# Norm statistics by a 128x128 block of ones, with root and reciprocal taken over all token columns in PSUM

## The chip, the cores and the metric

The kernel runs on one core of a Trainium2 chip. The metric is device time in microseconds (us) of one launch, and lower is better. The core has a matrix engine (TensorE, PE in the profile; its weight loads are PEld), VectorE (DVE), ScalarE (ACT), GpSimd (POOL) and SyncE (SP), which here issues the transfers. Each engine works through its own list of instructions in order and waits for the others only at semaphores.

## What is computed

A two-layer backbone over 512 latent tokens and 256 context tokens, 1024 features wide, all in fp32. The layers are built from the same step, a root-mean-square norm with a gain, followed by a scale and a shift that depend on the conditioning vector:

```python
def rms_norm(x, g):
    xf = x.astype(jnp.float32)
    y = xf * lax.rsqrt(jnp.mean(xf * xf, axis=-1, keepdims=True) + EPS)
    return (y * g.astype(jnp.float32)).astype(x.dtype)

def modulate(x, g, shift, scale):
    return rms_norm(x, g) * (1 + scale) + shift

for l in range(DEPTH):                     # DEPTH = 2
    ...
    a_lat = modulate(x, norm1_g[l], mod_lat[0], mod_lat[1])
    a_ctx = modulate(h, norm1_g[l], mod_ctx[0], mod_ctx[1])
    m_lat, m_ctx = token_mixers(a_lat, a_ctx, ...)
    x = x + mod_lat[2] * m_lat
    x = x + mod_lat[5] * sq_relu_mlp(modulate(x, norm2_g[l], mod_lat[3], mod_lat[4]), w_ff1[l], w_ff2[l])
    ...
```

So there are four norms: before the input projection and before the MLP, in each of two layers. The last one has no context tokens, since the output holds latent tokens only.

## The kernel before

The residual stream stands in `X`, 128 features on the partitions, 8 feature tiles (`KT`), and 768 token columns (`COLS`: 512 latent, `LAT`, then 256 context). Weights come in fp32 units of 128x1024 (`raw`); ACT rounds each to a high part (`Whi`), POOL subtracts to get the low part (`Wlo`), and every product is three matmuls: high by high, high by low, low by high. The activations are split the same way into `Ahi` and `Alo`, by the norm itself.

The order on each engine is written out by hand. The four norms are numbered n = 0 to 3. Each goes through the same chain:

- ACT squares each feature tile of `X` into `sqb` (L562). DVE adds the first seven squares into one tile, `sq_sums`, a part of `Ab` (`sq_add`, L868); the eighth stays in `sqb`.
- PE sums over the 128 features on the partitions (`stats`, `token_sums`, L1249). The squares are the stationary operand, 128 tokens at a time, and a 128x1 column of ones is the moving one; the result is one PSUM column per token tile, tokens on the partitions: `psS` 128x6, or 128x4 in the last norm. This is done for `sq_sums` and again for `sqb`.
- ACT takes the root of these 128x6 values (L568), DVE the reciprocal (L838), both in the small tile `rstd`.
- PE spreads them back to token columns that are the same on all partitions: one transpose per token tile of a column broadcast to 128x128 (`spread`, L1234 with `rstd`), latent tokens into the PSUM bank `ps6`, context tokens into `ps7`.
- DVE multiplies each feature tile of `X` by its gain and by `ps7` or `ps6` (L855 for 256 context columns, L857 for 512 latent ones). ACT adds the shift and rounds to `Ahi` (L575, L576), and DVE (even tiles, L844 and L846) or POOL (odd tiles, L457) makes `Alo`. The first matmul of the next stage (L1353, or L1566 in the MLP) waits for the first `Alo`.

`ps6` and `ps7` also serve the modulation vectors. PE writes partial sums there (`mod_sums`), DVE reduces them (`mod_reduce`, L822 and L825) and counts `mod_evac`. Before, `spread` waits for that count, since it is the first of the norm's steps that writes these banks. Before norm 1 the last `mod_reduce` stands on DVE behind the last `sq_add` and ahead of the reciprocal.

Of the kernel before, what the change touches and what calls it, by code (L numbers as in the profile page):

```python
# [17 lines left out]
P = 128  # L18
D, DEPTH, LAT, CTX = 1024, 2, 512, 256
KT = D // P  # L20
NT, NL = (LAT + CTX) // P, LAT // P
COLS = LAT + CTX
# [33 lines left out]
def build(nc, a):  # L56
    fp32, f32r = mybir.dt.float32, mybir.dt.float32r
    ALU, ACT, AX = mybir.AluOpType, mybir.ActivationFunctionType, mybir.AxisListType.X
# [3 lines left out]
    def sb(name, shape, dt=fp32):  # L62
        return stack.enter_context(nc.sbuf_tensor(name, shape, dt))
# [37 lines left out]
    Whi = sb("Whi", [P, 2, UE], f32r)  # L101
    Wlo = sb("Wlo", [P, 2, UE], f32r)
    ident = sb("ident", [P, P])
    ones = sb("ones", [P, 1])
    rstd = sb("rstd", [P, 2, NT])
    warm = sb("warm", [P, 1])
    identr = sb("identr", [P, P], f32r)
    maskr = sb("maskr", [P, 2, P], f32r)
# [30 lines left out]
    epst = sb("epst", [P, 1])  # L139


    def pb(name, n):
        return stack.enter_context(nc.psum_tensor(name, [P, n], fp32))

    psA, psB, psS = pb("psA", 1024), pb("psB", 1024), pb("psS", 1024)
    pair = [psA, psB]
    ps6, ps7 = pb("ps6", 512), pb("ps7", 512)
    tokbank = [psA[:, 0:512], psA[:, 512:1024], psB[:, 0:512], psB[:, 512:1024], psS[:, 0:512], psS[:, 512:1024]]

    names = """consts_in x_in tmp_in stored rows_T par_ready csil_ready mod_pe mod_first mod_used mod_step modp_ready mod_red mod_evac xT_ready x_ready  # L150
        stat_sq stat_done sq_sum rt_sqrt rstd_ready rb_ready dve a_full a_hi a_lo_even a_lo_odd hi_done lo_done unit_done proj_ready p_ready qk_var qk_sqrt
        q_ready k_ready rq_ready rk_ready tr_ready tr_evac za_evac zb_evac zc_evac y_ready y_hi y_lo
        kz_ready kv_ready st_ready sc_ready md_ready sd_zero xq_ready gg_ready rot_step ret_ready g_cent g_sq g_gate g_var g_sqrt g_inv v_sum v_ready ro_ready rT_ready rT_hi rT_lo
        kq_hi kl_ready kl_zero qb_hi qb_lo s_ready s_max s_exp pt_ready pt_evac pv_ready es_in es_out ao_ready aoT_ready aoT_hi aoT_lo
# [2 lines left out]
    S = {n: stack.enter_context(nc.semaphore(n)) for n in names}  # L157
# [5 lines left out]
    evac_index, n = {}, 0  # L163
# [4 lines left out]
    TT = [NT, NL]  # L168
# [366 lines left out]
    def _(act):  # L535
# [28 lines left out]
        def norm(n, cols):  # L564

            l, g = n // 2, n % 2
            act.wait_ge(S["stat_done"], n + 1)
            nc.scalar.activation(rstd[:, 0, 0:cols // P], psS[:, 0:cols // P], ACT.Sqrt, scale=1.0 / D, bias=epst[:, 0:1]).then_inc(S["rt_sqrt"], 1)  # L568
            for k in range(KT):
                act.wait_ge(S["a_full"], 8 * n + k + 1)  # L570
                sh = modT[:, l, 24 * g + k, :]
                for dst in (Ahi[:, k, :], norm_at(k)) if k % 2 else (Ahi[:, k, :],):

                    if cols > LAT:
                        nc.scalar.activation(dst[:, LAT:cols], norm_at(k)[:, LAT:cols], ACT.Identity, bias=sh[:, 1:2])  # L575
                    last = nc.scalar.activation(dst[:, 0:LAT], norm_at(k)[:, 0:LAT], ACT.Identity, bias=sh[:, 0:1])  # L576
                last.then_inc(S["a_hi"], 1)
# [204 lines left out]
    def _(dve):  # L782
        V = nc.vector
# [50 lines left out]
        def norm(l, k, cols):  # L834

            n = 2 * l + k
            dve.wait_ge(S["rt_sqrt"], n + 1)
            V.reciprocal(rstd[:, 1, 0:cols // P], rstd[:, 0, 0:cols // P]).then_inc(S["rstd_ready"], 1)  # L838

            def low(j):  # L840
                dve.wait_ge(S["a_hi"], 8 * n + j + 1)
                x, sh = norm_at(j), modT[:, l, 24 * k + j, :]
                if cols > LAT:
                    V.scalar_tensor_tensor(out=Alo[:, j, LAT:cols], in0=x[:, LAT:cols], scalar=sh[:, 1:2], in1=Ahi[:, j, LAT:cols],  # L844
                                           op0=ALU.add, op1=ALU.subtract)
                V.scalar_tensor_tensor(out=Alo[:, j, 0:LAT], in0=x[:, 0:LAT], scalar=sh[:, 0:1], in1=Ahi[:, j, 0:LAT],  # L846
                                       op0=ALU.add, op1=ALU.subtract).then_inc(S["a_lo_even"], 1)

            dve.wait_ge(S["rb_ready"], n + 1)
            for j in range(KT):  # L850
                if j >= 4 and j % 2:
                    dve.wait_ge(*a_lo(n, j - 4))
                x = norm_at(j)
                if cols > LAT:
                    V.scalar_tensor_tensor(out=x[:, LAT:cols], in0=X[:, j, LAT:cols], scalar=gs[:, l, k, j, 1:2], in1=ps7[:, 0:cols - LAT],  # L855
                                           op0=ALU.mult, op1=ALU.mult)
                V.scalar_tensor_tensor(out=x[:, 0:LAT], in0=X[:, j, 0:LAT], scalar=gs[:, l, k, j, 0:1], in1=ps6[:, 0:LAT],  # L857
                                       op0=ALU.mult, op1=ALU.mult).then_inc(S["a_full"], 1)
                if j % 2:
                    low(j - 1)  # L860
# [369 lines left out]
    def _(pe):  # L1230
        mm = nc.tensor.matmul

        def tr(out, in_, n=P):
            return nc.tensor.transpose(out, in_, ident[0:n, 0:n])  # L1234

        def mod_sums(used, w, wd, acc):

            pe.wait_ge(used, w + 1)
            pe.wait_ge(S["mod_step"], wd * 3 + 3)
            for s, ps in ((0, ps6), (1, ps7)):  # L1240
                for t in range(4):
                    last = tr(ps[:, t * P:(t + 1) * P], acc[:, s, t * P:(t + 1) * P])
            last.then_inc(S["modp_ready"], 1)

        def token_sums(n, squares, tiles_, first, last_):

            for t in range(tiles_):

                ins = mm(psS[:, t:t + 1], squares[:, t * P:(t + 1) * P], ones[:, :], start=(first and t == 0), stop=(last_ and t == tiles_ - 1))  # L1249
            return ins  # L1250

        def stats(n, tiles_):

            pe.wait_ge(S["sq_sum"], 6 * n + 6)
            token_sums(n, sq_sums, tiles_, True, False)
            pe.wait_ge(S["stat_sq"], 8 * n + 8)
            token_sums(n, sqb[:, 1], tiles_, False, True).then_inc(S["stat_done"], 1)

        def spread(n, tiles_):

            pe.wait_ge(S["rstd_ready"], n + 1)
            for t in range(tiles_):
                last = tr(ps6[:, t * P:(t + 1) * P] if t < NL else ps7[:, (t - NL) * P:(t - NL + 1) * P], rstd[:, 1, t:t + 1].to_broadcast([P, P]))
            last.then_inc(S["rb_ready"], 1)

        def fourier_weights(l):

# [37 lines left out]
        for m in range(KT):  # L1305
            if m >= 2:
                pe.wait_ge(S["x_ready"], m - 1)
            for t in range(NT):
                last = tr(pair[m % 2][:, t * P:(t + 1) * P], Xin[:, t, m * P:(m + 1) * P])
# [5 lines left out]
                mod_sums(S["mod_first"], 3, 3, maccs[0])  # L1315
        pe.wait_ge(S["mod_evac"], 1)
        mod_sums(S["mod_first"], 7, 7, maccs[1])
        stats(0, NT)
        pe.wait_ge(S["mod_evac"], 4)

        for l in range(DEPTH):
            u0, uf = l * UL, l * UL + UP + UO
            tiles = proj_tiles(l)
            pe.wait_ge(S["prep_wd"], 2 * l + 2)
            spread(2 * l, NT)

            for u in range(UP):
                g = u // 4
                n = GROUPS[g][1]
# [241 lines left out]
            for u in range(UO):  # L1571
# [5 lines left out]
                if l == 0 and u in (5, 7):  # L1577
# [1 line left out]
                    i = u // 2 - 2  # L1579
                    pe.wait_ge(S["mod_evac"], 10 + i)  # L1580
                    mod_sums(S["mod_used"], LATE - MOD0 + 4 * i + 3, 32 + 4 * i + 3, maccs[i])
            stats(2 * l + 1, TT[l])
            if l == 0:
                pe.wait_ge(S["mod_evac"], 12)
            spread(2 * l + 1, TT[l])


            pe.wait_ge(S["lo_done"], uf + 2)
            for k in range(KT):
# [53 lines left out]
            for k in range(4):  # L1643
                uu = uf + 60 + k
                pe.wait_ge(S["lo_done"], uu + 1)
                for o in range(2):
# [4 lines left out]
                    offs = [i * 256 + o * P for i in range(CHUNK)]  # L1651
                    tile(pair[m % 2], uu % 2, offs, Hhi[:, 1], Hlo[:, 1]).then_inc(S["lin_ready"], 1)
            if l == 0:
                stats(2, NT)

        pe.wait_ge(S["resid_done"], 144)
# [78 lines left out]
```

## Time and profile before

| what | value |
|---|---|
| median of 3 runs | 1805.34 us (1792.31 to 1811.72) |
| profiled execution, its own time | 1804.67 us |
| its span | 1802.9 us |
| PE busy | 1653.7 us, 92% |
| DVE busy | 1071.2 us, 59% |
| ACT busy | 572.3 us, 32% |
| POOL busy | 565.0 us, 31% |

PE is busy for nearly all of the span, so its gaps are what other engines can lose or save. The chain that ended last gives PE 56%, "issue" 19%, DVE 15% and ACT 4%. A norm is one of the few places where PE stands idle while a short chain of the other engines runs.

### The profile page before, as it was taken

To read this page: it belongs to the slowest core of one execution; us is meant where nothing else is said; L and a number is where in the kernel's file an instruction comes from. 1 tells how busy PE (TensorE), PEld (TensorE's weight loads), DVE (VectorE), ACT (ScalarE), POOL (GpSimd) and SP (SyncE) were. 2 spreads that over 40 slices of the span, in tenths; PEclk is the share of its full clock that TensorE was granted. 3 is DMA by queue.
4 is the path that set the end of the run, shared out by engine and by line. 5 is a ranking of instruction groups with operands and counts; after the bars stand their busy time and mean duration, and the time that the engine had idled before them with its cause. 6 is when DMAs were issued, how large, how long until landed. Compare 5 with 4: busy or idle time off the path is not lost.

```text
span 1802.9 us, 23460 instructions
## 1 busy us (share of the span) xinstructions
PE 1653.7 (92%) x8944; PEld 1425.2 (79%) x8944; DVE 1071.2 (59%) x1534; ACT 572.3 (32%) x912; POOL 565.0 (31%) x312
## 2 busy tenths in 40 slices
PE   6799778998979998998999997998899899999998
PEld 6678567897868887887888886887798678888887
DVE  3779975554856775766677437368453554444442
ACT  1531133563142121221211215323364442222221
POOL 0234546101232222222222233335301344444442
PEclk9999889898989998999999997998699899999999
DMA  7254411001413433444244111222000233333332
GB/s 269 70 168 146 130 36 42 1 1 36 135 60 104 129 105 96 133 116 125 71 140 117 59 59 37 83 80 71 1 1 24 70 94 94 93 93 93 93 93 93
DMA packets 159407, 156.08 MB, mean 87 GB/s; under 512 B 6336, under 2 KB 123728, under 8 KB 159312
## 3 DMA queue, kind: packets, MB, share of 16 engines
q1 hardware_dynamic: 159312, 154.72, 28.3%
q8 instruction: 70, 1.15, 0.3%
q14 instruction: 25, 0.20, 0.0%
HBM read 152.61 MB, written 2.10 MB: 86 GB/s over the span
## 4 chain that ended last, share of the span: by engine, by line
PE 56%; issue 19%; DVE 15%; ACT 4%; POOL 3%; DMA 2%; SPq 0%; POOLq 0%; DVEq 0%; ACTq 0%
PE psA L1566 18%; PE psB L1566 17%; PE ps L1535 4%; POOL Wlo L430 3%; PE psS L1234 2%; DVE Tb L813 2%; DVE scr L968 2%; DVE macc L813 2%; PE psS L1294 1%; PE ps L1234 1%; PE psS L1459 1%; DMA modraw<-in_w_mod_dram 1%; DVE Ab L1174 1%; PE psS L1249 1%; DVE scr L962 1%
## 5 line engine op out<-in xcount | busy, mean ns | idle before, releaser
L430 POOL TENSOR_TENSOR Wlo<-raw,Whi 128x1024 fp32r<-128x1024 f32 x172 | 419.1, 2437 | 1075.0 <-ACT Whi L541 1075.0
L541 ACT ACTIVATE Whi<-raw 128x1024 fp32r<-128x1024 f32 x180 | 190.8, 1061 | 782.2 <-PE psB L1566 329.6
L1174 DVE TENSOR_TENSOR Ab<-Tb 128x768 f32<-128x768 f32 (+1 forms) x64 | 162.0, 2531 | 189.3 <-ACT Tb L750 189.3
L813 DVE SCALAR_TENSOR_TENSOR macc<-modraw,csil,macc 128x512 f32<-128x512 f32 x224 | 193.3, 925 | 8.3 <-DMA modraw<-in_w_mod_dram 8.2
L1566 PE MATMUL psA<-Ahi,Whi 128*128 128x512 f32 x480 | 150.2, 368 | 21.8 <-POOL Wlo L430 9.1
L1566 PE MATMUL psA<-Ahi,Wlo 128*128 128x512 f32 x480 | 148.5, 364 | 3.4 <-issue 3.4
L1566 PE MATMUL psA<-Alo,Whi 128*128 128x512 f32 x480 | 148.2, 363 | 0.0
L1566 PE MATMUL psB<-Ahi,Whi 128*128 128x512 f32 x480 | 145.0, 356 | 0.0
L1566 PE MATMUL psB<-Ahi,Wlo 128*128 128x512 f32 x480 | 144.7, 355 | 0.0
L1566 PE MATMUL psB<-Alo,Whi 128*128 128x512 f32 x480 | 144.5, 355 | 0.0
L1566 PE MATMUL psA<-Hhi,Whi 128*128 128x512 f32 (+1 forms) x384 | 117.2, 359 | 14.0 <-DVE X L951 14.0
L1566 PE MATMUL psA<-Hhi,Wlo 128*128 128x512 f32 (+1 forms) x384 | 115.4, 355 | 0.0
L1566 PE MATMUL psA<-Hlo,Whi 128*128 128x512 f32 (+1 forms) x384 | 115.4, 354 | 0.0
L1566 PE MATMUL psB<-Hhi,Wlo 128*128 128x512 f32 (+1 forms) x384 | 115.4, 354 | 0.0
L1566 PE MATMUL psB<-Hlo,Whi 128*128 128x512 f32 (+1 forms) x384 | 115.3, 354 | 0.0
L1566 PE MATMUL psB<-Hhi,Whi 128*128 128x512 f32 (+1 forms) x384 | 115.2, 354 | 0.0
L1566 PEld LDWEIGHTS psA<-Ahi,Whi 128*128 128x128 f32 x480 | 82.0, 196 | 37.7 <-issue 14.7
L752 ACT ACTIVATE Hhi<-Ab 128x768 fp32r<-128x768 f32 (+1 forms) x64 | 47.4, 740 | 166.2 <-DVE Ab L1174 166.2
L1566 PEld LDWEIGHTS psA<-Ahi,Wlo 128*128 128x128 f32 x480 | 81.8, 195 | 17.9 <-issue 4.2
L1566 PEld LDWEIGHTS psA<-Alo,Whi 128*128 128x128 f32 x480 | 81.8, 195 | 14.0
L951 DVE SCALAR_TENSOR_TENSOR X<-psA,modT,X 128x512 f32<-128x512 f32 x72 | 53.5, 744 | 65.8 <-PE psA L1566 65.8
L1566 PEld LDWEIGHTS psB<-Alo,Whi 128*128 128x128 f32 x480 | 79.4, 189 | 13.5
(293 smaller groups left out, 3311.6 us busy)
## 6 DMA issues: line engine op xcount, KB each, us to landing
raw<-in_w_ff_dram SPq DMA_DIRECT2D x128, 512.0 KB, 4.1
modraw<-in_w_mod_dram SPq DMA_DIRECT2D x80, 512.0 KB, 4.1
raw<-in_w_in_dram SPq DMA_DIRECT2D x36, 512.0 KB, 3.7
modst<-in_w_mod_dram SPq DMA_DIRECT2D x16, 512.0 KB, 5.2
raw<-in_w_out_dram SPq DMA_DIRECT2D x16, 512.0 KB, 4.0
modraw<-in_dft_lat_dram SPq DMA_DIRECT2D x8, 257.0 KB, 3.6
Xin<-in_x_dram SPq DMA_DIRECT2D x4, 512.0 KB, 10.1
out_dram<-outs SPq DMA_DIRECT2D x4, 512.0 KB, 3.0
```

What stands on the lines that cost most here:

```text
L430: nc.gpsimd.tensor_tensor(Wlo[:, s, :], raw[:, s, :], Whi[:, s, :], ALU.subtract).then_inc(S["lo_done"], 1)
L541: nc.scalar.activation(Whi[:, slot, :], raw[:, slot, :], ACT.Copy).then_inc(S["hi_done"], 1)
L752: nc.scalar.activation(Hhi[:, hpar, k, 0:CW[l]], Ab[:, k % 2, 0:CW[l]], ACT.Copy).then_inc(S["h_hi"], 1)
L813: ins = V.scalar_tensor_tensor(out=acc[:, s, :], in0=src[:, kk * MCH:(kk + 1) * MCH], scalar=col, in1=acc[:, s, :], op0=ALU.mult, op1=ALU.add)
L951: V.scalar_tensor_tensor(out=X[:, m, 0:LAT], in0=pair[p][:, 0:LAT], scalar=modT[:, l, 8 * chunk + m, 0:1], in1=X[:, m, 0:LAT], op0=ALU.mul ...
L962: link(V.tensor_tensor(scr[:, 1, 0:n].rearrange("p (h d) -> p h d", h=nh), v3, bc(C, 1, [P, nh, HD]), ALU.mult))
L968: link(V.tensor_tensor(os[:, :, q, f, :], vs[:, :, q, 1 - f, :], bc(ss[:, q, f, :], 1, [P, nh, i]), ALU.mult))
L1174: V.tensor_tensor(Ab[:, k % 2, 0:w], Tb[:, k % 2, 0:w], Tb[:, k % 2, 0:w], ALU.mult).then_inc(S["h_full"], 1)
L1234: return nc.tensor.transpose(out, in_, ident[0:n, 0:n])
L1249: ins = mm(psS[:, t:t + 1], squares[:, t * P:(t + 1) * P], ones[:, :], start=(first and t == 0), stop=(last_ and t == tiles_ - 1))
L1535: last = mm((ps6, ps7)[b % 2][:, h * HD:(h + 1) * HD], PTs[:, it % 2, i * P:(i + 1) * P], Pk[:, kt, P + (h // 4) * HD:P + (h // 4 + 1) * H ...
L1566: last = mm(dst[:, c0:c0 + cn], wt, x[:, i, c0:c0 + cn], start=f, stop=e)
```

## The change

The column of ones becomes a 128x128 block of ones, and the operands of the statistics matmuls change places: the ones are stationary, and the squares are streamed as 512 latent and 256 context columns. Each output column then holds its token's sum on all 128 partitions, straight in `ps6` and `ps7`. The root (ACT) and the reciprocal (DVE) are taken in place over all of these columns, and the spreading transposes, their semaphore `rb_ready` and the tile `rstd` go. As the statistics now write `ps6` and `ps7`, the waits for `mod_evac` and `prep_wd` that stood ahead of `spread` stand ahead of `stats`.

```diff
--- before.py
+++ after.py
@@ -101,8 +101,7 @@
     Whi = sb("Whi", [P, 2, UE], f32r)
     Wlo = sb("Wlo", [P, 2, UE], f32r)
     ident = sb("ident", [P, P])
-    ones = sb("ones", [P, 1])
-    rstd = sb("rstd", [P, 2, NT])
+    ones = sb("ones", [P, P])
     warm = sb("warm", [P, 1])
     identr = sb("identr", [P, P], f32r)
     maskr = sb("maskr", [P, 2, P], f32r)
...
@@ -565,7 +564,9 @@
 
             l, g = n // 2, n % 2
             act.wait_ge(S["stat_done"], n + 1)
-            nc.scalar.activation(rstd[:, 0, 0:cols // P], psS[:, 0:cols // P], ACT.Sqrt, scale=1.0 / D, bias=epst[:, 0:1]).then_inc(S["rt_sqrt"], 1)
+            if cols > LAT:
+                nc.scalar.activation(ps7[:, 0:cols - LAT], ps7[:, 0:cols - LAT], ACT.Sqrt, scale=1.0 / D, bias=epst[:, 0:1])
+            nc.scalar.activation(ps6[:, 0:LAT], ps6[:, 0:LAT], ACT.Sqrt, scale=1.0 / D, bias=epst[:, 0:1]).then_inc(S["rt_sqrt"], 1)
             for k in range(KT):
                 act.wait_ge(S["a_full"], 8 * n + k + 1)
                 sh = modT[:, l, 24 * g + k, :]
@@ -835,7 +836,9 @@
 
             n = 2 * l + k
             dve.wait_ge(S["rt_sqrt"], n + 1)
-            V.reciprocal(rstd[:, 1, 0:cols // P], rstd[:, 0, 0:cols // P]).then_inc(S["rstd_ready"], 1)
+            if cols > LAT:
+                V.reciprocal(ps7[:, 0:cols - LAT], ps7[:, 0:cols - LAT])
+            V.reciprocal(ps6[:, 0:LAT], ps6[:, 0:LAT]).then_inc(S["rstd_ready"], 1)
 
             def low(j):
                 dve.wait_ge(S["a_hi"], 8 * n + j + 1)
@@ -846,7 +849,7 @@
                 V.scalar_tensor_tensor(out=Alo[:, j, 0:LAT], in0=x[:, 0:LAT], scalar=sh[:, 0:1], in1=Ahi[:, j, 0:LAT],
                                        op0=ALU.add, op1=ALU.subtract).then_inc(S["a_lo_even"], 1)
 
-            dve.wait_ge(S["rb_ready"], n + 1)
+            dve.wait_ge(S["rstd_ready"], n + 1)
             for j in range(KT):
                 if j >= 4 and j % 2:
                     dve.wait_ge(*a_lo(n, j - 4))
@@ -1244,10 +1247,9 @@
 
         def token_sums(n, squares, tiles_, first, last_):
 
-            for t in range(tiles_):
-
-                ins = mm(psS[:, t:t + 1], squares[:, t * P:(t + 1) * P], ones[:, :], start=(first and t == 0), stop=(last_ and t == tiles_ - 1))
-            return ins
+            if tiles_ > NL:
+                mm(ps7[:, 0:COLS - LAT], ones[:, :], squares[:, LAT:COLS], start=first, stop=last_)
+            return mm(ps6[:, 0:LAT], ones[:, :], squares[:, 0:LAT], start=first, stop=last_)
 
         def stats(n, tiles_):
 
@@ -1255,13 +1257,6 @@
             token_sums(n, sq_sums, tiles_, True, False)
             pe.wait_ge(S["stat_sq"], 8 * n + 8)
             token_sums(n, sqb[:, 1], tiles_, False, True).then_inc(S["stat_done"], 1)
-
-        def spread(n, tiles_):
-
-            pe.wait_ge(S["rstd_ready"], n + 1)
-            for t in range(tiles_):
-                last = tr(ps6[:, t * P:(t + 1) * P] if t < NL else ps7[:, (t - NL) * P:(t - NL + 1) * P], rstd[:, 1, t:t + 1].to_broadcast([P, P]))
-            last.then_inc(S["rb_ready"], 1)
 
         def fourier_weights(l):
 
@@ -1315,15 +1310,13 @@
                 mod_sums(S["mod_first"], 3, 3, maccs[0])
         pe.wait_ge(S["mod_evac"], 1)
         mod_sums(S["mod_first"], 7, 7, maccs[1])
+        pe.wait_ge(S["mod_evac"], 4)
         stats(0, NT)
-        pe.wait_ge(S["mod_evac"], 4)
 
         for l in range(DEPTH):
             u0, uf = l * UL, l * UL + UP + UO
             tiles = proj_tiles(l)
             pe.wait_ge(S["prep_wd"], 2 * l + 2)
-            spread(2 * l, NT)
-
             for u in range(UP):
                 g = u // 4
                 n = GROUPS[g][1]
@@ -1579,11 +1572,9 @@
                     i = u // 2 - 2
                     pe.wait_ge(S["mod_evac"], 10 + i)
                     mod_sums(S["mod_used"], LATE - MOD0 + 4 * i + 3, 32 + 4 * i + 3, maccs[i])
+            if l == 0:
+                pe.wait_ge(S["mod_evac"], 12)
             stats(2 * l + 1, TT[l])
-            if l == 0:
-                pe.wait_ge(S["mod_evac"], 12)
-            spread(2 * l + 1, TT[l])
-
 
             pe.wait_ge(S["lo_done"], uf + 2)
             for k in range(KT):
@@ -1651,6 +1642,7 @@
                     offs = [i * 256 + o * P for i in range(CHUNK)]
                     tile(pair[m % 2], uu % 2, offs, Hhi[:, 1], Hlo[:, 1]).then_inc(S["lin_ready"], 1)
             if l == 0:
+                pe.wait_ge(S["prep_wd"], 4)
                 stats(2, NT)
 
         pe.wait_ge(S["resid_done"], 144)
```

**Order of PE at norm 1**, in front of the first MLP matmuls of layer 0 (`Ab` and `sqb` hold the squares, `Tb` a modulation sum). Before:

```order
1653 L1234 MATMUL ps<-ident,Tb 128x128 [waits mod_step,mod_used,mod_evac]
1654 L1234 MATMUL ps<-ident,Tb 128x128 x7
1655 L1249 MATMUL psS<-ones,Ab 128x1 [waits sq_sum]
1656 L1249 MATMUL psS<-ones,Ab 128x1 x5
1657 L1249 MATMUL psS<-ones,sqb 128x1 [waits stat_sq]
1658 L1249 MATMUL psS<-ones,sqb 128x1 x5
1659 L1234 MATMUL ps<-ident,rstd 128x128 [waits rstd_ready,mod_evac]
1660 L1234 MATMUL ps<-ident,rstd 128x128 x5
1661 L1566 MATMUL psA<-Ahi,Whi 128x512 [waits a_lo_even,lo_done]
```

With the change:

```order
1651 L1237 MATMUL ps<-ident,Tb 128x128 [waits mod_step,mod_used,mod_evac]
1652 L1237 MATMUL ps<-ident,Tb 128x128 x7
1653 L1251 MATMUL ps<-Ab,ones 128x256 [waits sq_sum,mod_evac]
1654 L1252 MATMUL ps<-Ab,ones 128x512
1655 L1251 MATMUL ps<-sqb,ones 128x256 [waits stat_sq]
1656 L1252 MATMUL ps<-sqb,ones 128x512
1657 L1559 MATMUL psA<-Ahi,Whi 128x512 [waits a_lo_even,lo_done]
```

Twelve matmuls and six transposes become four matmuls, and the wait for `mod_evac` moves from the transposes to the first of the sums.

**Order of DVE at norm 1.** Before:

```order
496 L868 TENSOR_TENSOR Ab<-Ab,sqb 128x768 [waits sq_sum,stat_sq]
497 L822 TENSOR_REDUCE modT<-ps 128x4 [waits modp_ready]
498 L822 TENSOR_REDUCE modT<-ps 128x4
499 L825 TENSOR_TENSOR modT<-modT,bmodT 128x8 [waits mod_red]
500 L838 RECIPROCAL rstd<-rstd 128x6 [waits rt_sqrt]
501 L855 SCALAR_TENSOR_TENSOR Tb<-X,gs,ps 128x256 [waits rb_ready]
```

With the change:

```order
497 L871 TENSOR_TENSOR Ab<-Ab,sqb 128x768 [waits sq_sum,stat_sq]
498 L823 TENSOR_REDUCE modT<-ps 128x4 [waits modp_ready]
499 L823 TENSOR_REDUCE modT<-ps 128x4
500 L826 TENSOR_TENSOR modT<-modT,bmodT 128x8 [waits mod_red]
501 L840 RECIPROCAL ps<-ps 128x256 [waits rt_sqrt]
502 L841 RECIPROCAL ps<-ps 128x512
503 L858 SCALAR_TENSOR_TENSOR Tb<-X,gs,ps 128x256 [waits rstd_ready]
```

One reciprocal over 6 columns becomes two over 256 and 512 columns. `mod_reduce` keeps its place, and PE's statistics now wait for it.

## Rows read from the trace of the kernel before

**Rows 1.** The page, busy time, share of the span and instructions.
```profile
PE 1653.7 (92%) x8944; PEld 1425.2 (79%) x8944; DVE 1071.2 (59%) x1534; ACT 572.3 (32%) x912; POOL 565.0 (31%) x312
```

**Rows 2.** The chain that ended last, at norm 0: start us, us, what.
```profile
64.95 0.97 DVE Ab L868
65.96 5.29 PE psS L1249 x24
71.28 0.28 ACT rstd L568
71.65 0.20 DVE rstd L838
71.98 1.53 PE ps L1234 x6
73.54 0.48 DVE Tb L855
```

**Rows 3.** The same chain at norm 1.
```profile
502.44 3.91 PE psS L1249 x24
506.38 0.28 ACT rstd L568
508.57 0.48 DVE Tb L855
```

**Rows 4.** Timeline at norm 1: start us, us, engine, line, work.
```profile
503.62 0.17 DVE L825 TENSOR_TENSOR modT<-modT,bmodT 128x8 f32<-128x8 f32 x1
```

**Rows 5.** The chain at norm 2.
```profile
1098.42 5.29 PE psS L1249 x24
1103.73 0.28 ACT rstd L568
1105.99 0.48 DVE Tb L855
```

**Rows 6.** The chain at norm 3, latent tokens alone.
```profile
1424.62 2.73 PE psS L1249 x16
1427.38 0.27 ACT rstd L568
1429.06 0.76 DVE Tb L857
```

**Rows 7.** Groups of DVE by line and shape: count, busy us, mean ns.
```profile
L838 DVE RECIPROCAL rstd<-rstd 128x6 f32<-128x6 f32 x3 | 0.6, 191 | 8.6 <-ACT rstd L568 8.6
L1110 DVE RECIPROCAL gst<-gst 128x8 f32<-128x8 f32 x10 | 2.0, 204 | 2.3 <-ACT gst L697 2.2
L989 DVE RECIPROCAL srt<-srt 128x60 f32<-128x60 f32 x2 | 1.1, 526 | 17.7 <-ACT srt L643 17.7
```

**Rows 8.** Timeline of PE in layer 0's Fourier mixing.
```profile
289.40 3.60 PE L1430 MATMUL psA<-Zs,WCS 128*128 128x512 f32 x8
```

**Rows 9.** Groups of ACT by line and shape, reading PSUM.
```profile
L635 ACT ACTIVATE Pu<-psB 128x256 f32<-128x256 f32 x4 | 1.5, 384 | 4.2 <-PE psB L1355 4.2
L635 ACT ACTIVATE Pk<-psB 128x512 f32<-128x512 f32 x4 | 2.4, 599 | 3.0 <-PE psB L1355 3.0
L720 ACT ACTIVATE Pb<-psA,nm 128x512 f32<-128x512 f32 x16 | 11.0, 688 | 0.1
```

**Rows 10.** Busy time by stretch: PE, PEld, DVE, ACT, POOL, then PEclk (granted), DMA.
```profile
502.00:504.00 2.00, 1.56 (x14) 1.56 (x15) 1.76 (x4) 0.28 (x1) 0.00 (x0) 1.00 0.38 104
504.00:506.00 2.00, 2.00 (x12) 2.00 (x11) 0.00 (x0) 0.00 (x0) 0.00 (x0) 0.50 0.91 227
1118.00:1120.00 2.00, 2.00 (x9) 1.64 (x8) 1.86 (x4) 2.00 (x5) 1.38 (x1) 0.90 0.00 0
1434.00:1436.00 2.00, 2.00 (x6) 1.56 (x6) 1.87 (x4) 1.59 (x4) 1.29 (x1) 0.54 0.00 0
```

**Rows 11.** Timeline: PE's first matmuls after norms 2 and 3.
```profile
1109.61 0.77 PE L1353 MATMUL psA<-Whi,Ahi 128*128 128x512 f32 x1 [3.66 <-DVE Alo L846]
...
1431.49 0.77 PE L1566 MATMUL psA<-Ahi,Whi 128*128 128x512 f32 x1 [2.47 <-DVE Alo L846]
```

More of the change, by code:

```diff
@@ L150, in build @@
     names = """consts_in x_in tmp_in stored rows_T par_ready csil_ready mod_pe mod_first mod_used mod_step modp_ready mod_red mod_evac xT_ready x_ready
-        stat_sq stat_done sq_sum rt_sqrt rstd_ready rb_ready dve a_full a_hi a_lo_even a_lo_odd hi_done lo_done unit_done proj_ready p_ready qk_var qk_sqrt
+        stat_sq stat_done sq_sum rt_sqrt rstd_ready dve a_full a_hi a_lo_even a_lo_odd hi_done lo_done unit_done proj_ready p_ready qk_var qk_sqrt
         q_ready k_ready rq_ready rk_ready tr_ready tr_evac za_evac zb_evac zc_evac y_ready y_hi y_lo
@@ L1581, in _ @@
                     mod_sums(S["mod_used"], LATE - MOD0 + 4 * i + 3, 32 + 4 * i + 3, maccs[i])
-            stats(2 * l + 1, TT[l])
             if l == 0:
                 pe.wait_ge(S["mod_evac"], 12)
-            spread(2 * l + 1, TT[l])
+            stats(2 * l + 1, TT[l])
             pe.wait_ge(S["lo_done"], uf + 2)
```

## The prediction

> **What bounds the kernel now.** I read the page first: PE is busy for 92% of the span [rows 1], so only PE's gaps can move the end by much, and the four norms are such gaps. Then I read the chain that ended last, at each norm [rows 2, 3, 5, 6]. In all four it runs through every step that the change touches: the last sum of squares on DVE, the 24 (or 16) records of the statistics on PE, root, reciprocal, spreading transposes, and the first scaling on DVE. Nothing else ends later there, so what is added to this chain moves the end by as much. The reader should see how short the two middle steps are: the root takes 0.28 us and the reciprocal 0.20 us, since they work on 6 columns. Last I read the groups by shape, for the prices of the new forms [rows 7 to 9], and the granted clock [rows 10].
>
> **The statistics matmuls: no change in length.** Each norm had 2 x 6 matmuls on 128 stationary columns; an fp32 matmul is two records, hence x24. At norms 0 and 2 they take 5.29 us [rows 2, 5]. Now 2 x (512 + 256) columns are streamed against the ones. The nearest row is an fp32 128x512 matmul: 8 records in 3.60 us [rows 8], so about 0.43 us a record and 0.86 us a matmul. That stretch is at the full clock. The statistics run at half of it: at norm 1 the granted clock falls from 1.00 to 0.50, that is from 2.4 to 1.2 GHz, while they run [rows 10], and norms 0 and 2 need 5.29 us for what norm 1, partly at full clock, does in 3.91 us. At half clock a 512-column matmul is 1.71 us and a 256-column one 0.86, the set 2.57, both sets 5.14 and with the last one's tail 5.3. Norms 0 and 2: 0. Norm 3: 2 x 1.71 at half clock, 2 x 0.86 at full, against 2.73 us now [rows 6], which mixes both; 0. The bounds are half clock all through (+0.8) and full clock all through (-1.0).
>
> **Norm 1's statistics start later.** Their wait for the modulation banks moves ahead of them. DVE gets there at 503.62 + 0.17 = 503.79 us [rows 4], while the statistics start at 502.44 us [rows 3]: +1.4 us. By then the clock has fallen, or falls at once, so the whole 5.3 us are at half clock where 3.91 us stood: +1.4 us. Together +2.8 us; the bounds are +1.4 (full clock kept for as long as now) and +2.9. At norms 0, 2 and 3 the moved waits cost nothing: the modulation reduce of norm 0 stands on DVE ahead of the last sum of squares, norm 2's preparation is long done, and norm 3 has none.
>
> **From the root's start to the first scaling.** I replace this stretch whole. Now it is 73.54 - 71.28 = 2.26 us at norm 0 [rows 2], 2.19 at norm 1 [rows 3], 2.26 at norm 2 [rows 5] and 1.68 at norm 3 [rows 6]. The transposes, 1.53 us, are within it.
> - Root on ACT, in place in PSUM, 256 and then 512 columns. Plain copies out of PSUM take 0.384 and 0.599 us, one with an operand per partition 0.688 us for 512 [rows 9]. No row writes PSUM from ACT. The two overlap a little; 1.1 us, between 0.98 (the plain copies in sequence) and 1.3 (both dearer). Norm 3, 512 columns alone: 0.69 us.
> - Reciprocal on DVE, the term that decides. Three sizes stand in the trace: 191 ns for 6 columns, 204 for 8, 526 for 60 [rows 7]. From 8 to 60 columns it rises by 322 ns for 52, so 6.2 ns a column; from 6 to 8 by 6.5 ns a column. What is left is 0.154 us fixed. 256 columns: 0.154 + 256 x 0.0062 = 1.74 us. 512 columns: 0.154 + 512 x 0.0062 = 3.33 us. Together 5.0 us with a small overlap, where 0.20 stood; norm 3: 3.33 us. Both sizes are extrapolated and in PSUM, where no reciprocal stands, so the lower bound is that the rise flattens to what other DVE work shows (the 256-column scaling, 0.48 us [rows 2], and the 512-column one, 0.76 us [rows 6]: 1.24 for both), and the upper one a third above my figure (6.6 us). I take the slope, since it holds over a tenfold range of sizes on this very operation.
> - Hand-overs, about 0.13 us (71.65 less the root's end at norm 0 [rows 2], and DVE's wait for itself).
>
> Sum for 768 columns: 1.1 + 5.0 + 0.13 = 6.25 us, against 2.26: +4.0 us. For norm 3: 0.69 + 3.33 + 0.1 = 4.1 us, against 1.68: +2.4 us.
>
> The page "VectorE: DVE Perf Modes" of the Trainium skill has a rule that speaks for a far cheaper reciprocal. Its section on the TRN2 errata gives VectorE work out of PSUM as 120 cycles and one per column, at 0.96 GHz; by that an estimate for both sizes is 1.05 us, and the four norms would add little. The trace disagrees already at 60 columns: that rule (58 cycles from SBUF) gives 0.12 us, the row 0.526. The same page, in its walkthrough of the pipeline, says that the reciprocal is an iterative divide with a repeat count of 8; read as 8 cycles a column, an estimate for both sizes is 6.4 us and more, and the kernel would be some 6 us slower than I say. The measured slope stands between the two readings.
>
> **What hides the rest.** The larger block of ones is set by POOL in the first microseconds, long before anyone uses it. Weight units for the stage behind the norm are already split when it ends and no further ones can be loaded meanwhile, so a longer norm gives no work back later. PE has restarted at half clock after every norm, so its restart is not colder than it was.
>
> **The sum.** Norm 0 +4.0, norm 1 +2.8 + 4.0, norm 2 +4.0, norm 3 +2.4: +17.2 us. On the profiled execution's own 1804.7 us (span 1802.9) this is 1821.9 us; the median of the runs, 1805.3, is 0.7 us away, so the same figure serves. About 1%, 18 us, is what a measurement of this kernel can tell from no change. The forecast is just inside it: 1822 us.
>
> **Rivals.**
> - *The reciprocal is not linear* in columns at these sizes. At the lower bound above, DVE takes 1.24 us in place of 5.0 (norm 3: 0.76 in place of 3.33), which takes 3 x 3.8 + 2.6 = 14 us off: 1808 us. For it: no large reciprocal is in the trace. Against it: the slope. Chance 0.06. The PSUM formula in the errata section of "VectorE: DVE Perf Modes" in the Trainium skill would give nearly this time.
> - *The streaming statistics lift the clock.* They keep PE dense for 5 us, and PE's clock rose after 4 to 9 us of dense work behind the norms: from 1431.49 us to within 1434 to 1436 at norm 3, and from 1109.61 to within 1118 to 1120 at norm 2 [rows 10, 11]. If the second set of each norm runs at full clock, 3 x 1.3 + 0.9 = 5 us are saved, and if norm 1 keeps its clock another 1.4: 1816 us. Against it: the rise came late, and PE then stands idle for about 10 us, so nothing carries over. Chance 0.12.
> - *The clock comes back later* behind the longer gap, on the other side of the line. After norm 3 PE ran at half clock for about 4.4 us, after norm 2 for about 8.8 [rows 10, 11]. Each further microsecond at half clock costs 0.5 us once PE bounds the stage. If two norms take the long end in place of the short one this adds 2 x 2.2 = 4.4 us: 1826 us, slower by 1.2%. It decides from 0.9 us on, since that is all that parts the forecast from the line. For it: the phase of the rise is shifted in every norm. Against it: in the first microseconds behind a norm, DVE and ACT bound the stage and not PE, as the gap of 3.66 us in front of PE's first matmul shows [rows 11]. Chance 0.16.
> - *The reciprocal is dearer in PSUM* (the upper bound, +1.6 us in three norms, +1.1 in the fourth): 1828 us. Chance 0.05.
> - *Faster than before*: it would take the flat reciprocal and the lifted clock together. Chance 0.01.
>
> **How the numbers follow.** 0.60 is left for the forecast itself. Its own range is 1817 to 1828 us, from the terms' bounds (roots 0.2 us each way, statistics of norms 1 and 3) and from the runs before, which lie 20 us apart with a median that can be off by several. The line is at 1823.4 us, so I split this case 0.35 within 1% and 0.25 slower. Within 1%: 0.35 + 0.06 + 0.12 = 0.53; slower: 0.25 + 0.16 + 0.05 = 0.46; faster 0.01. The range that should hold the time 8 times in 10 reaches from the lifted clock with some spread of the runs, 1811, to the dear reciprocal with the same, 1832.
>
> **What would show it.** In the profile of the changed kernel the two reciprocals should read about 1.74 and 3.33 us, the roots 0.4 to 0.5 and 0.69 us, the statistics of norm 0 about 5.3 us, and those of norm 1 should start behind the modulation reduce. From the last sum of squares to the first scaling, norm 0 should take 11.6 us in place of 7.6, norm 1 about 13 in place of 6.2. The prediction is wrong if the large reciprocal is under 1 us, if the stage behind a norm keeps a different length than it has now, or if time outside the norms moves by more than a few microseconds.

## The result, and the profile after

The changed kernel takes 1812.5 us in the median of 20 runs (1806.0 to 1831.0), the kernel before 1805.2 us (1792.3 to 1813.7). The ratio is 1.0056, with a 95% interval of 1.0032 to 1.0079, so about 10 us (6 to 14) were added; the two medians alone lie 7 us apart. A second set of 12 runs, in experiment 1, gave 1.0097 (1.0065 to 1.0129), 17 us (12 to 23). The forecast was 1822 us, just inside 1%. Runs in a slow state are left out of the ratios: two of the kernel before, at 1821.2 and 1819.9 us, and one of after_keep_p68 in experiment 7, at 2356.6 us and a granted clock of 0.656.

The first thing to look at is norm 0 in the chain that ended last of the changed kernel (start us, us, what). It answers to [rows 2].

```profile
65.98 1.19 PE ps L1251 x2
67.17 1.71 PE ps L1252 x2
68.87 0.85 PE ps L1251 x2
69.73 0.87 PE ps L1252 x2
70.60 0.02 issue
70.62 0.45 ACT ps L568
71.07 0.59 ACT ps L569
...
71.75 1.77 DVE ps L840
73.52 3.22 DVE ps L841
76.74 0.02 issue
76.76 0.48 DVE Tb L858
```

From the root's start to the first scaling it is 6.14 us, where 2.26 stood; the reciprocals alone are 5.0. The groups of DVE by shape (count, busy us, mean ns, idle before) give both sizes, to be held against 1.74 and 3.33 us of the prediction and [rows 7]:

```profile
L841 DVE RECIPROCAL ps<-ps 128x512 f32<-128x512 f32 x4 | 13.3, 3319 | 4.6 <-ACT ps L569 4.6
L840 DVE RECIPROCAL ps<-ps 128x256 f32<-128x256 f32 x3 | 5.3, 1766 | 14.4 <-ACT ps L569 14.4
```

Norm 1 in the timeline (start, length, engine, line, work, idle before) shows the moved wait, against [rows 3, 4]. PE's first sum starts 0.05 us behind DVE's L826, the end of the modulation reduce:

```profile
523.72 0.17 DVE L826 TENSOR_TENSOR modT<-modT,bmodT 128x8 f32<-128x8 f32 x1
523.94 1.22 PE L1251 MATMUL ps<-Ab,ones 128*128 128x256 f32 x2 [4.97 <-DVE modT L826]
524.96 1.92 PE L1252 MATMUL ps<-Ab,ones 128*128 128x512 f32 x2
526.66 0.76 PE L1251 MATMUL ps<-sqb,ones 128*128 128x256 f32 x2
527.26 1.02 PE L1252 MATMUL ps<-sqb,ones 128*128 128x512 f32 x2
528.32 0.45 ACT L568 ACTIVATE ps<-ps,epst 128x256 f32<-128x256 f32 x1 [5.94 <-PE ps L1252]
```

Norm 3 in the chain, against [rows 6]:

```profile
1440.25 3.79 PE ps L1252 x4
1444.07 0.67 ACT ps L569
1444.76 3.38 DVE ps L841
1448.14 0.02 issue
1448.16 0.76 DVE Tb L860
```

I cut both timelines at the same instructions of PE and subtracted. From the end of the last sum of squares to PE's first matmul behind the norm, the norms took 11.2, 9.8, 11.2 and 6.9 us before, and take 14.6, 15.5, 15.4 and 10.4 us now: +3.3, +5.7, +4.2, +3.5, in all 16.6 us. But three stages that hold nothing of the change also moved, by 7 to 17 us each (retention is a chain of small matmuls in the token mixer, and the MLP row is cut at its first matmul that reads the hidden tile `Hhi`):

| stage | before | after | difference |
|---|---|---|---|
| four norms | 39.2 | 55.9 | +16.6 |
| retention, layer 0 | 23.2 | 39.9 | +16.7 |
| retention, layer 1 | 23.8 | 16.3 | -7.5 |
| MLP from its first matmul on `Hhi` to norm 2's sums, layer 0 | 512.7 | 506.0 | -6.7 |
| span | 1802.9 | 1822.3 | +19.4 |

Layer 0's retention stage by stretch (PE, PEld, DVE, ACT and POOL busy, then the granted clock), the kernel before first, then the changed one:

```profile
297.50:320.70 23.20, 22.04 (x201) 20.38 (x201) 17.48 (x31) 6.59 (x14) 14.57 (x18) 1.00 0.01 1
```

```profile
300.70:340.60 39.90, 39.90 (x201) 37.32 (x201) 17.92 (x31) 6.97 (x15) 16.18 (x19) 0.51 0.00 1
```

The same 201 matmul records, at 2.4 GHz in the one and 1.2 GHz in the other. In layer 1 it is the profile of the kernel before that is the odd one: 23.8 us, where each of the 13 other profiles has 15.9 to 16.3. So the profiled 1822.3 us, though almost the forecast, is that in part by luck: the two retention stages, of which the forecast knew nothing, add 9.2 us between these two profiles. The experiments are there to part the norms from the rest.

### The profile page after: what moved, and what is told of

It reads as the page before. It is cut to its first block, busy times and chain, and to the rows that moved or that the text cites. A ratio compares the mean times of both kernels' runs of the same rounds, so it can differ in the third digit from the quotient of the medians.

```text
span 1822.3 us, 23302 instructions
## 1 busy us (share of the span) xinstructions
PE 1657.2 (91%) x8862; PEld 1418.3 (78%) x8862; DVE 1084.3 (60%) x1537; ACT 574.9 (32%) x915; POOL 563.5 (31%) x312
## 4 chain that ended last, share of the span: by engine, by line
PE 55%; issue 19%; DVE 15%; ACT 4%; POOL 4%; DMA 2%; SPq 0%; POOLq 0%; DVEq 0%; ACTq 0%
PE psA L1559 18%; PE psB L1559 17%; PE ps L1528 4%; POOL Wlo L429 3%; PE psS L1237 2%; DVE scr L971 2%; DVE Tb L814 2%; PE psS L1452 2%; DVE macc L814 1%; PE psS L1289 1%; DVE Ab L1177 1%; PE ps L1237 1%; DVE scr L965 1%; DVE ps L841 1%; PE psS L1466 1%
## 5 line engine op out<-in xcount | busy, mean ns | idle before, releaser
L1559 PE MATMUL psA<-Ahi,Whi 128*128 128x512 f32 x480 | 150.2, 368 | 31.5 <-DVE Alo L849 16.3
L1559 PEld LDWEIGHTS psB<-Ahi,Wlo 128*128 128x128 f32 x480 | 79.4, 189 | 13.7
```

The costliest lines, as they stand in the source:

```text
L1559: last = mm(dst[:, c0:c0 + cn], wt, x[:, i, c0:c0 + cn], start=f, stop=e)
```

## The experiments

**1. The change once more.** No edit.

> The change itself, once more, beside the kernel before. In its profile the four norms are longer by 3.2, 6.5, 4.1 and about 4.5 us (18.7 us in all from the first sum to PE's restart, and norm 1's late start), yet 20 runs gave a ratio of 1.0056, about +10 us (+6 to +14). Theory A (the norms' length passes through whole, and stages far from the norms, the retention stage above all, take another length by chance in each execution): the norms read the same as in the first profile within 0.5 us, the two retention stages take any of 16, 23 or 40 us, and the time is 8 to 20 us above before. Theory B (part of the added time is always given back behind the norms): the norms read the same, and the stages behind them are shorter than before's in this profile as well.

1824.6 us in the median of 12 runs, before 1802.2; ratio 1.0097 (1.0065 to 1.0129). In its profile root's start to first scaling reads as in the first one (6.1 us in norms 0 to 2, 4.1 in norm 3), the retention stages 39.8 and 15.9 us, the MLP stage 507.2. The four norms take 56.8 us in place of 55.9. Norm 1 is 1.2 us longer, more than the 0.5 us that theory A allowed, since here all of its sums ran at half clock. (The expectation's +6.5 and +4.5 us for norms 1 and 3 are too large for the first profile; the cut above gives +5.7 and +3.5.) B's condition, a shorter MLP stage than in the first profile of before, holds too, so something there is not chance.

**2. Only a pause, in the kernel before.**

```diff
             dve.wait_ge(S["rb_ready"], n + 1)
+            V.reciprocal(sqb[:, 0, 0:620 if cols > LAT else 364], sqb[:, 0, 0:620 if cols > LAT else 364])
             for j in range(KT):
```

> The kernel before with nothing but a pause on DVE: behind the wait for the spread columns it takes a reciprocal over 620 columns of a tile nobody reads any more (364 in norm 3). By the slope of the reciprocal this is 3.9 us in norms 0 to 2 and 2.3 us in norm 3, 14 us in all, which is what the change adds between the root's start and the first scaling; the statistics on PE stay as they were. Theory A (length passes through whole): +14 us, and the same in the profile's norms. Theory B (part is given back behind a longer norm): +5 to +8 us. Theory C (what the change gives back comes from the streamed statistics and the clock they leave behind): +14 us here, too, so that only the next kernel parts it from A.

1823.4 us, ratio 1.0103 (1.0073 to 1.0133): +19 us (13 to 24), so B falls. In the profile the four norms are 15.5 us longer than before's, and the four stages next behind them together 0.3 us shorter, so nothing is given back there. A reciprocal over 620 columns reads 4028 ns in its profile, one over 364 reads 2428, both on the line of 6.2 ns a column. Layer 0's retention stage was the long one here, too (39.8 us), so the time alone does not say how much of the 19 us is the pause.

**3. No reciprocal.** This kernel leaves the reciprocal out and so computes another output.

```diff
-            if cols > LAT:
-                V.reciprocal(ps7[:, 0:cols - LAT], ps7[:, 0:cols - LAT])
-            V.reciprocal(ps6[:, 0:LAT], ps6[:, 0:LAT]).then_inc(S["rstd_ready"], 1)
...
-            nc.scalar.activation(ps6[:, 0:LAT], ps6[:, 0:LAT], ACT.Sqrt, scale=1.0 / D, bias=epst[:, 0:1]).then_inc(S["rt_sqrt"], 1)
+            nc.scalar.activation(ps6[:, 0:LAT], ps6[:, 0:LAT], ACT.Sqrt, scale=1e-8, bias=epst[:, 0:1]).then_inc(S["rt_sqrt"], 1)
```

> The changed kernel without the reciprocals, and with another scale in the root to keep numbers finite: the streams are scaled by something else than 1/rms, so the output is another one. It takes 5.0 us out of norms 0 to 2 and 3.3 out of norm 3, 18.4 us. Theory A: 18 us under the changed kernel, 0 to +1 us against before. Theory B: only 8 to 12 us under the changed kernel. Theory C: under before by 6 to 10 us, since the gift of the streamed statistics stays.

1789.8 us, ratio 0.9939 (0.9910 to 0.9969): 11 us under before, and 35 under the change of experiment 1, measured together. The profiles of the two lie 41.3 us apart, 19.3 of it in the norms and 16.6 in layer 0's retention stage, which is long in the one and short in the other.

**4. Root and reciprocal in one ACT function.**

```diff
-            nc.scalar.activation(ps6[:, 0:LAT], ps6[:, 0:LAT], ACT.Sqrt, scale=1.0 / D, bias=epst[:, 0:1]).then_inc(S["rt_sqrt"], 1)
+            nc.scalar.activation(ps6[:, 0:LAT], ps6[:, 0:LAT], ACT.Abs_reciprocal_sqrt, scale=1.0 / D, bias=epst[:, 0:1]).then_inc(S["rt_sqrt"], 1)
```

(the same for `ps7`, and for the small call that loads the function's table early; the reciprocals are gone)

> The changed kernel with root and reciprocal in one ACT function (the absolute reciprocal root, over the same 256 and 512 columns), and none on DVE. The output is the reference's. Norms 0 to 2 lose 5.0 us, norm 3 loses 3.3 against the changed kernel, if the function costs what the root costs (0.45 and 0.65 us); if it is dearer, that shows in its rows. Theory A: 18 us under the changed kernel, within 1 us of before. Theory C: 6 to 10 us under before.

1788.6 us, ratio 0.9940 (0.9910 to 0.9971), the same as without a reciprocal. The function costs what the root did, in the groups of ACT:

```profile
L569 ACT ACTIVATE ps<-ps,epst 128x512 f32<-128x512 f32 x4 | 2.6, 655 | 4.1 <-PE ps L1248 4.1
L568 ACT ACTIVATE ps<-ps,epst 128x256 f32<-128x256 f32 x3 | 1.3, 448 | 16.9 <-PE ps L1248 16.9
```

From the root's start to the first scaling it is now 1.1 us, 5.0 less than in the change. Both kernels lie 5 to 16 us under before by the intervals, as C had it and not A. But in the profiles the norms are only 0.8 to 1.8 us shorter than before's in norms 0 and 2, 0.9 us longer in norm 1 and level in norm 3. The larger part is in layer 1's retention stage, 16 us where before's profile has 23.8, and again in the MLP stage, 504.6 and 505.7 us, where before has 512.7. The delayed kernel, with before's own PE program, has 508.9 there.

**5. Matmuls in PE's gap ahead of retention**, in both kernels and in experiment 4.

```diff
+            pe.wait_ge(S["st_ready"], (l + 1) * 4 * NST_E)
+            keep_clock(ps7, 10)
             pe.wait_ge(S["y_lo"], 2 * l + (2 if l == 0 else 1))
```

> The kernel before with ten matmuls of 512 columns, whose result nobody reads, in PE's gap of 2.75 us ahead of each retention stage. In the profiles so far the retention stage of layer 0 took 23.2 us where PE entered it at full clock (before, norecip, arsq) and 39.9 us where the granted clock fell to 0.50 about 1 us behind its start (the change, twice, and the delayed kernel). Theory A1 (the clock falls in this gap in some executions, and then stays at half until the stage ends): layer 0's stage takes 23 us in the profile, the time is under before by the share of its executions that had the long stage, 2 to 6 us, and the times lie closer together. Theory A2 (it falls elsewhere): no change, within 2 us of before.

1780.3 us, ratio 0.9860 (0.9828 to 0.9892): 25 us under before, far more than the 2 to 6 that I expected.

> The changed kernel with the same ten matmuls ahead of each retention stage. Theory A1: layer 0's retention stage takes 23 us in the profile and not 39.9, the time is 8 to 15 us under that of the change, and the distance to the kernel before with the same matmuls is the norms' 17 to 19 us alone. Theory A2: still 39.9 us in the profile, and no gain. Theory C (the streamed statistics give something back): the distance is under 12 us.

1806.1 us, ratio 1.0005 (0.9988 to 1.0023), and the 12 runs lie within 7 us, where those of the change spread over 23. It is 26 us above before_keep, where I had 17 to 19. Its retention stage, by stretch, is the short one at full clock:

```profile
302.10:325.20 23.10, 21.94 (x199) 20.28 (x200) 17.48 (x31) 6.58 (x14) 14.52 (x18) 1.00 0.01 1
```

> The changed kernel with root and reciprocal in one ACT function, and the same ten matmuls ahead of each retention stage. Both theories: 18.4 us under the changed kernel with these matmuls, by the norms' lengths (5.0 us three times and 3.4). Against the kernel before with them: 0 to 1 us by the norms of the profiles (the change 18.7 us above before, less 18.4).

1789.4 us, ratio 0.9915 (0.9883 to 0.9946), 16.6 us under the change with the same matmuls, where both theories had 18.4; against before with them it is 9 us above, where I had 0 to 1. Its runs lie within 6 us in place of 24, and its median is no lower.

A1 holds for the retention stage: kept busy in that gap, layer 0's stage took 23.2 us in every profile (7 of 7 with these matmuls), and the spread of the runs closed. It does not explain the 25 us of before_keep. The subtraction of stages does: the two profiles lie 21.7 us apart, and its MLP stage in layer 0 takes 492.7 us, 20.0 less than before's; the change's takes 505.7 with the same edit. Layer 1's retention stage (15.9 us in place of 23.8) makes up the rest, less some 6 us that other stages lost. Here is PE at a turn of the MLP loop in the timeline of the kernel before:

```profile
691.93 1.03 PE L1234 MATMUL ps<-ident,macc 128*128 128x128 f32 x8
696.75 1.00 PE L1566 MATMUL psA<-Ahi,Whi 128*128 128x512 f32 x2 [3.78 <-issue]
697.55 0.84 PE L1566 MATMUL psA<-Alo,Whi 128*128 128x512 f32 x2
```

and in that of before_keep, where the instructions and the waits of the loop are the same:

```profile
693.72 1.04 PE L1234 MATMUL ps<-ident,macc 128*128 128x128 f32 x8
694.51 0.59 PE L1568 MATMUL psA<-Ahi,Whi 128*128 128x512 f32 x2
694.93 0.51 PE L1568 MATMUL psA<-Alo,Whi 128*128 128x512 f32 x2
```

3.78 us in which the timeline shows PE waiting for nothing; the loop has three rounds and two turns, and both turns have such a gap. (Of the 20 gaps of this kind in the ten profiles that have them, 10 read "issue" and 10 are put down to POOL's `Wlo`; but in before_keep PE goes on while POOL still works on that `Wlo`, so PE does not need it there.) The first matmuls behind it run at half clock (0.84 us for a pair in place of 0.51). What differs between the two programs is how much stands in PE's program ahead of the loop. I counted the records of PE (its sequencer's among them) and of its weight loads up to the stage's first matmul, which lies in the loop's first round, always the same distance behind its start: 5956 before, 5976 with the ten matmuls, 5868 in the change, 5888 in the change with them.

**6. The statistics of norms 1 and 3 in two other banks**, on top of experiment 4 and of the ten matmuls.

```diff
+    def norm_banks(n):
+        return (psS[:, 0:LAT], psS[:, LAT:COLS]) if n % 2 else (ps6[:, 0:LAT], ps7[:, 0:COLS - LAT])
...
-            if l == 0:
-                pe.wait_ge(S["mod_evac"], 12)
             stats(2 * l + 1, TT[l])
```

> As the last one, and norms 1 and 3 take the two free banks of psS in place of ps6 and ps7, so that norm 1's statistics no longer wait for the modulation reduce. By the profiles that wait cost 1.2 to 1.4 us, and up to 1.3 us more if the first set then ran at full clock: 1 to 3 us under the last kernel, if the norm's late start was on the path, and none if not. If all adds up, this is the fastest kernel of the study, some 15 us under before.

1788.6 us, ratio 0.9900 (0.9869 to 0.9932): 0.9 us under its sibling arsq_keep, within the noise of both. The timeline of norm 1 shows that the wait itself is gone: the sums start 0.05 us behind DVE's last sum of squares, and the reduce runs beside them:

```profile
503.03 2.47 DVE L873 TENSOR_TENSOR Ab<-Ab,sqb 128x768 f32<-128x768 f32 x1 [0.74 <-ACT sqb L565]
...
505.55 0.96 PE L1254 MATMUL psS<-Ab,ones 128*128 128x256 f32 x2 [3.56 <-DVE Ab L873]
```

In the sibling they start 1.46 us behind it:

```profile
497.63 2.47 DVE L867 TENSOR_TENSOR Ab<-Ab,sqb 128x768 f32<-128x768 f32 x1 [0.74 <-ACT sqb L561]
...
501.56 1.22 PE L1247 MATMUL ps<-Ab,ones 128*128 128x256 f32 x2 [4.97 <-DVE modT L826]
```

So the term of 1.4 us is right, and norm 1 takes 9.3 us in place of 10.7. A gain of that size cannot be told by the times of six runs.

**7. PE's program lengthened where PE idles anyway**, at its very start.

```diff
+        pe.wait_ge(S["pool_init"], 1)
+        for i in range(22):
+            mm(psA[:, 0:1], WCS[:, 0, 0, :], WCS[:, 0, 0, 0:1], start=True, stop=True)
         pe.wait_ge(S["consts_in"], 10 * 16)
```

(22, 17 or 5 of these matmuls, four records each)

> The changed kernel with the ten matmuls ahead of each retention stage, and 22 fp32 matmuls of one column at PE's start, where it waits for its first data: 88 PE instructions. With them PE has 5976 instructions ahead of layer 0's MLP loop, as many as before_keep, which ran that stage (first second-half matmul of the MLP to norm 2's statistics) in 492.7 us without PE's two idle gaps of 3.4 to 3.9 us at the loop's turns, where all the others took 503 to 513. Theory P (the gaps at the loop's turns depend on how many instructions stand ahead of the loop): no such gaps, 492.7 us, and 13 us under after_keep, 1793 us, 13 to 15 us above before_keep. Theory Q (they come from the longer norms or the clock): the stage takes 505 us and the time stays at 1806 us.

1794.2 us, ratio 0.9962 (0.9938 to 0.9985), where P had 1793. The gaps at the turns are gone:

```profile
702.80 1.04 PE L1237 MATMUL ps<-ident,macc 128*128 128x128 f32 x8
703.59 0.59 PE L1564 MATMUL psA<-Ahi,Whi 128*128 128x512 f32 x2
```

and the stage takes 492.9 us.

> The same with 17 such matmuls, 68 instructions: 5956 ahead of the loop, as in the kernel before. Theory P: the gaps of the kernel before, two of 3.5 to 3.9 us and two of 1.3 to 2.1 behind them, 509 to 513 us for the stage, 3 to 7 us above after_keep. That would be the part of the added time that the change got back: its PE program is 88 instructions shorter there. Theory Q: as after_keep, 1806 us.

1811.5 us in the median of 11 runs, ratio 1.0041 (1.0017 to 1.0066), measured together with the last one. With five one-column matmuls fewer it is 17.3 us slower:

```profile
701.63 1.03 PE L1237 MATMUL ps<-ident,macc 128*128 128x128 f32 x8
706.34 0.61 PE L1564 MATMUL psA<-Ahi,Whi 128*128 128x512 f32 x2 [3.68 <-issue]
706.78 0.51 PE L1564 MATMUL psA<-Alo,Whi 128*128 128x512 f32 x2
709.26 1.01 PE L1564 MATMUL psA<-Ahi,Wlo 128*128 128x512 f32 x2 [1.96 <-issue]
```

Here is also a second gap, of 1.96 us, 3 us behind the first. The kernel before has it, and the change has not. The stage takes 511.7 us.

> The kernel before with 5 one-column fp32 matmuls at PE's start, 20 instructions, and nothing else: 5976 ahead of the loop. Theory P: layer 0's MLP stage in 492.7 us and not 512.7 (508.9 in the delayed kernel, which has the same PE program), so 16 to 20 us under before; the retention stages stay with their chance. Theory Q: as before.

1780.2 us, ratio 0.9891 (0.9845 to 0.9938): 20 us under before for five matmuls of one column. The stage takes 492.9 us.

> The kernel with root and reciprocal in one ACT function, the statistics of norms 1 and 3 in psS and the ten matmuls ahead of retention, with 22 one-column matmuls at the start: 5975 instructions ahead of the loop. Theory P: 13 us under the same without them, 1776 us, and 4 to 6 us under before_keep by the norms (each 0.8 to 1.1 us shorter than before's); 29 us under before, the fastest of the study. Theory Q: 1789 us.

1780.6 us, ratio 0.9868 (0.9827 to 0.9909), 8 us under the same without them, where I had 13, and level with before_keep and before_p20, where I had 4 to 6 less. Its MLP stage takes 493.1 us. Of the three, before_keep has the lowest ratio (0.9860), but they cannot be told apart.

P holds four times in four, in both kernels, and in the change both ways:

| PE records up to the stage | kernels | MLP stage, us |
|---|---|---|
| 5868 | the change (twice), norecip, arsq | 506.0, 507.2, 505.7, 504.6 |
| 5887 or 5888 | after_keep, arsq_keep, best | 505.7, 503.0, 505.8 |
| 5956 | before, delay, after_keep_p68 | 512.7, 508.9, 511.7 |
| 5975 or 5976 | before_keep, before_p20, after_keep_p88, best_p88 | 492.7, 492.9, 492.9, 493.1 |

What PE waits for in these gaps stands among the DMA queues, where transfers that load instructions are a kind of their own. The page of the kernel before and that of before_keep have (packets, MB, share of the 16 engines):

```profile
q8 instruction: 70, 1.15, 0.3%
```

```profile
q8 instruction: 53, 0.87, 0.2%
```

From 700 to 970 us, most of the loop's second and third rounds, the first has 15 of these and the second none. Over the whole stage there are 28 in the three kernels at 5956, 27 in the seven at 5868 to 5888, and 10 in the four at 5975 or 5976, in which the loop's instructions are loaded in its first round and not again. In each of the 20 gaps one such transfer, of 16 KB, starts 0.6 to 1.3 us behind the gap's start, and PE goes on 2.7 to 3.0 us later. So PE waits there for instructions; that they are its own is inferred from these times, since the view names no engine. Layer 1's MLP loop is free in all 14 profiles: no such transfer in its second and third rounds, no such gap at its turns, and 322.5 us from its first matmul on `Hhi` to the end in 13 of them. Why the loop is loaded again at one count and not at another is not shown.

## Why the prediction was right, and where not

- **The time** lies in the range, and within 1% was the likeliest class. The forecast of 1822 us is 10 us too high, and 1812.5 is only 1.5 us above the range's lower end, which stood there for a lifted clock and the spread of the runs and not for what took the 10 us off. In that the range held by luck. By a sign that the prediction itself named, it was wrong: time outside the norms moved by far more than a few microseconds.
- **The reciprocal**, the term that decided, was sized rightly: 1.77 and 3.32 us measured, 1.74 and 3.33 predicted. A slope taken from 8 and 60 columns held up to 620, in SBUF and in PSUM. The flat and the dear reciprocal both fall, and so does the reading of 8 cycles a column (6.4 us for both sizes; 5.1 measured).
- **Root's start to first scaling**: predicted +4.0 three times and +2.4; measured +3.9 three times and +2.4.
- **The statistics** were the loose term. Norm 0's sums take 4.6 us where 5.3 stood, since the clock rose while the last of them ran: the last pair of records takes 0.87 us where the same pair earlier takes 1.71. This is the rival of the lifted clock, in part, and the clock was down again at PE's restart. In norm 1 the sums took 4.3 us, not 5.3, for the same reason, so that norm gained 5.7 us and not 6.8; in experiment 1's profile they took 5.5 and the norm gained 6.9, so this is a matter of the execution. Norm 3's took 3.8 us in all profiles of the change, at half clock, where 2.7 stood: +1.1, where I took 0, and more than my bound of +0.8. From the last sum of squares to the first scaling, norm 0 took 10.9 us and norm 1 11.9, where I had 11.6 and 13.
- **The sum of the norms**: predicted +17.2 us, measured +16.6 between the two profiles. One kernel's norms differ a little from execution to execution, by the clock of their sums: 39.2, 40.6 and 41.1 us in before and its two variants of experiments 5 and 7, 55.6 to 56.8 us in the five profiles of the change. The pause of experiment 2 shows that a longer norm is not made up for in the stages next behind it.
- **What hides the rest** is the step that failed. I wrote that a longer norm gives no work back later, and looked only at work. The change makes PE's program 88 records shorter ahead of layer 0's MLP loop, and that loop's time depends on where it stands: the stage takes 504.6 to 507.2 us at the change's count, 508.9 to 512.7 at before's, 5 us less by the means. The norms' 16.6 us less these 5 are 11 to 12 us, and the 20 runs show 10 (6 to 14). With the count put back to before's, the change with the ten matmuls goes from a ratio of 1.0005 to 1.0041; the intervals overlap a little, and the plainer reading is the stage, 505.7 and 511.7 us. At the same count (5976) the change stands at 1794.2 us (ratio 0.9962) and the kernel before at 1780.2 (0.9891, measured together) and 1780.3 (0.9860): 13 and 18 us apart by the ratios, near the 15 to 16 us that their norms differ by in the profiles, and above the 10 of the verdict.
- **The clock behind the norm** moved the end by less than I allowed: PE's restart was at half clock as before, and the stages next behind the norms kept their lengths within 1.7 us. (The line at 1% is 1.4 us above the forecast by the prediction's own figures, not 0.9.) The clock mattered in a place that I did not look at, layer 0's retention stage. Without the ten matmuls it was the long one in all three profiles of kernels with longer norms, and the short one in before, norecip, arsq and before_p20. Whether a longer norm makes the fall likelier, or this was chance, seven profiles do not settle. The mean granted clock that every run has on record tells more on why the change's two sets of runs lie 10 and 17 us above before. In the first set 7 of 20 runs had 0.952 or less and took 1817 to 1831 us, and the other 13 took 1806 to 1815; in the second, 10 of 12 had 0.952 or less (1816 to 1837 us). Both profiles with the long stage are of this kind (0.948 and 0.947). So the sets differ in how often the clock was low; that it was low in the retention stage in the unprofiled runs, too, is not shown.

The page "VectorE: DVE Perf Modes" of the Trainium skill gives 120 cycles and one per column for VectorE out of PSUM into SBUF, in the section on the TRN2 errata. An estimate by that formula, at the page's 0.96 GHz, is 658 ns for 512 columns. The 3319 ns measured (in PSUM and back into it) are five times that, so the trace disagrees for this operation.

## What to carry to other kernels

An operation that costs nothing on a few columns can be priced at many by its slope, if the trace has it at two sizes; a layout that saves 1.5 us of transposes is not worth a reciprocal over 768 columns, which take 5 us to say what 6 columns say. Root and reciprocal in one function on ACT make the same layout cheap (1.1 us from the root's start to the first scaling). And when a verdict is under 1%, cut both profiles into stages first: here one stage that the edit never touches moved by as much as the edit, and two more by nearly half of it.

## What the hardware showed that I had not expected

- DVE's reciprocal takes 6.1 to 6.2 ns a column from 8 to 620 columns, 3319 ns for 512.
- A loop on PE can lose 3.4 to 4.1 us at each turn while instructions are loaded again, and up to 20 us over the stage with the second gaps and the half clock that follow, depending on how many instructions stand ahead of it. Of four counts, only 5976 (and 5975) was free of it. Which other counts are free was not tried. Twenty records more at PE's start made the kernel before 20 us faster (ratio 0.9891).
- Layer 0's retention stage, a chain of small matmuls, ran 23.2 us at 1.00 or 39.9 us at 0.51, with the same 201 matmul records. In the long case PE entered it at full clock behind 2.75 us of idle time, the granted clock fell about 1 us behind its start, and it came back only behind the stage. Ten matmuls in that idle time held the clock in all seven profiles that had them.
